# The head of a Mamba-2 trunk kernel: dt and unit 0 interleaved over the tiles of h, the dt and decay turns moved, group 0's exponentials later

## What is computed

```python
h = rms_norm(x, mix_pre_g)
zxbcdt = h @ w_in                       # z 2048, x 2048, B 1024, C 1024, dt 32 columns
xbc = silu(causal_dwconv(xbc, conv_w, conv_b))
dt = softplus(dt_raw + dt_bias)         # (tokens, 32 heads)
a = -dt * exp(a_log)
a_cs = cumsum(a)                        # within a chunk
lmat = exp(a_cs[l] - a_cs[s]), lower triangle
y_diag = (C @ B.T * lmat) @ (x * dt);  states = B.T @ (decay * x * dt);  y_off = C @ prev * exp(a_cs)
```

## Time and profile before

| | |
|---|---|
| median of 3 runs | 1354.79 us (1354.41 to 1354.86) |
| the profiled execution, its own time | 1355.58 us |
| its span, from the first to the last instruction | 1353.8 us |
| TensorE busy | 1333.6 us, 99% |
| VectorE, ScalarE, GpSimd busy | 57%, 42%, 2% |
| the chain that ended last | PE 83%, DVE 7%, ACT 5%, issue 2%, DMA 2% |

### The profile page before, as it was taken

The page is one execution under the profiler, slowest core; times in us unless marked ns, Lnnn a source line. Parts: engine busy times, 40 slices in busy tenths (PEclk is TensorE's granted clock), DMA queues, the critical chain, the costliest instruction groups (busy, mean ns, idle before and its releaser), DMA issues.

```text
span 1353.8 us, 15929 instructions
## 1 busy us (share of the span) xinstructions
PE 1333.6 (99%) x6474; PEld 1115.1 (82%) x6474; DVE 777.9 (57%) x1139; ACT 570.6 (42%) x875; POOL 24.4 (2%) x28
## 2 busy tenths in 40 slices
PE   8999999999999999999999999999999999999998
PEld 6878787877888988888888888888898888888886
DVE  4878778787624666666642266545466656664223
ACT  6666555666324534333331163222453333333112
POOL 0000000000000000000000000000000000000000
PEclk9999999999999999999999999999999999999999
DMA  4532234332242233333343313333223333334331
GB/s 148 162 109 70 89 107 125 110 112 74 79 140 63 63 109 109 94 96 103 97 126 102 115 47 96 104 96 112 91 63 109 108 95 93 94 103 130 93 109 62
DMA packets 181773, 135.70 MB, mean 100 GB/s; under 512 B 5645, under 2 KB 169893, under 8 KB 180677
## 3 DMA queue, kind: packets, MB, share of 16 engines
q1 hardware_dynamic: 181653, 134.62, 33.0%
q10 hardware_dynamic: 48, 0.07, 0.0%
HBM read 132.51 MB, written 2.16 MB: 99 GB/s over the span
## 4 chain that ended last, share of the span: by engine, by line
PE 83%; DVE 7%; ACT 5%; issue 2%; DMA 2%; SPq 0%; DVEq 0%
PE bank L850 17%; PE bank L851 17%; PE bank L852 17%; PE bank L911 9%; PE bank L913 9%; PE bank L912 9%; DMA w_raw<-in_ssd_w_in 2%; DVE mask L637 2%; DVE feat L709 1%; ACT w_hi L355 1%; ACT e_row L428 1%; DVE w_lo L586 1%; PE bank L888 1%; DVE feat L703 1%; ACT L413 1%
## 5 line engine op out<-in xcount | busy, mean ns | idle before, releaser
L850 PE MATMUL bank<-h_hi,w_hi 128*128 128x512 f32 (+1 forms) x1352 | 513.7, 380 | 0.0
L852 PE MATMUL bank<-h_lo,w_hi 128*128 128x512 f32 (+1 forms) x1352 | 511.0, 378 | 0.0
L851 PE MATMUL bank<-h_hi,w_lo 128*128 128x512 f32 (+1 forms) x1352 | 510.8, 378 | 0.0
L586 DVE TENSOR_TENSOR w_lo<-w_raw,w_hi 128x1024 fp32r<-128x1024 f32 x228 | 278.4, 1224 | 356.6 <-ACT w_hi L355 356.5
L355 ACT ACTIVATE w_hi<-w_raw 128x1024 fp32r<-128x1024 f32 x228 | 238.2, 1052 | 203.2 <-PE bank L913 172.8
L852 PEld LDWEIGHTS bank<-h_lo,w_hi 128*128 128x128 f32 x1352 | 254.3, 188 | 47.2
L850 PEld LDWEIGHTS bank<-h_hi,w_hi 128*128 128x128 f32 x1352 | 254.4, 188 | 46.5
L851 PEld LDWEIGHTS bank<-h_hi,w_lo 128*128 128x128 f32 x1352 | 254.4, 188 | 46.3
L911 PE MATMUL bank<-w_hi,hid_hi 128*128 128x512 f32 x416 | 162.4, 390 | 0.0
L913 PE MATMUL bank<-w_hi,hid_lo 128*128 128x512 f32 x416 | 161.9, 389 | 0.0
L912 PE MATMUL bank<-w_lo,hid_hi 128*128 128x512 f32 x416 | 161.8, 389 | 0.0
(11 more groups left out here) (146 smaller groups left out, 944.4 us busy)
## 6 DMA issues: line engine op xcount, KB each, us to landing
w_raw<-in_ffn_w_up SPq DMA_DIRECT2D x88, 512.0 KB, 3.8
w_raw<-in_ssd_w_in SPq DMA_DIRECT2D x48, 512.0 KB, 4.0
w_raw<-in_ffn_w_down SPq DMA_DIRECT2D x44, 512.0 KB, 3.5
w_raw<-in_sc_w_in SPq DMA_DIRECT2D x24, 512.0 KB, 3.7
acs_b<-acs_dram SPq DMA_DIRECT2D x8, 1024.0 KB, 6.2
w_raw<-in_ssd_w_out SPq DMA_DIRECT2D x16, 512.0 KB, 3.5
w_raw<-in_sc_w_out SPq DMA_DIRECT2D x8, 512.0 KB, 3.6
x_tok<-in_x SPq DMA_DIRECT2D x4, 512.0 KB, 4.9
```

What stands on the lines that cost most here:

```text
L586: nc.vector.tensor_tensor(w_lo[slot(u)][:], w_raw[:, u % 2, :], w_hi[slot(u)][:].bitcast(F32), ALU.subtract).then_inc(w_lo_done, 1)
L850: nc.tensor.matmul(dst, wh, xh, start=start, stop=False)
L851: nc.tensor.matmul(dst, wl, xh, start=False, stop=False)
L852: return nc.tensor.matmul(dst, wh, xl, start=False, stop=stop)
```

## The change

- dt: the high and the low weights stand side by side in one tile of 64 columns. Per tile of h two products (with h_hi and with h_lo) give 64 rows; the turn of dt multiplies these rows with a tile `pair` (two unit matrices over each other, made on GpSimd), which adds the halves. The cleared padding and its two memsets go.
- The split of dt's weight comes before the first tile of h on both engines; w_hi 0 and w_lo 0 come behind tile 1.
- TensorE runs the dt products as h_hi and h_lo of a tile come, and unit 0 in the same loop, two tiles behind (LAG). The second set of warm-up products between the transposes goes.
- The turns of dt and of the pages move from unit 0 to unit 1, the cumulative sums from unit 1 to unit 2.
- In group 0, ScalarE does conv_out 2 and conv_in 3 ahead of the exponentials; VectorE does conv 2 ahead of segments(0). The other groups keep their order.

```diff
@@ gpsimd
-            for part in (wdt_hi, wdt_lo):
-                pool.memset(part[:].bitcast(F32)[:, :, HEADS:], 0.0).then_inc(wdt_cleared, 1)
             pool.memset(ones[:], 1.0).then_inc(consts_done, 1)
+            pool.wait_ge(consts_done, 5)
+            pool.tensor_tensor(pair[:], ident[:, 0:HEADS], ident[:, HEADS:2 * HEADS], ALU.add).then_inc(pair_done, 1)
@@ scalar
+            act.wait_ge(wdt_landed, 16)
+            nc.scalar.activation(wdt[:, :, 0:HEADS], wdt_raw[:], ACT.Copy).then_inc(wdt_split, 1)
             act.wait_ge(par1_done, 1)
             for k in range(DT):
                 act.wait_ge(xn_turned, k + 1)
                 nc.scalar.activation(h_hi[:, k, :], bank[k % 6][:], ACT.Copy, scale=one(col_gain(MIX_PRE, 0, k))).then_inc(h0_hi_done, 1)
-                if k == 0:
-                    act.wait_ge(wdt_landed, 16)
-                    act.wait_ge(wdt_cleared, 2)
-                    nc.scalar.activation(wdt_hi[:, :, 0:HEADS], wdt_raw[:], ACT.Copy).then_inc(wdt_split, 1)
-                if k == 3:
+                if k == 1:
                     splits_to(1)
             splits_to(2)
             act.wait_ge(dt_row_mm, 1)
-            nc.scalar.copy(dt_row[:], bank[7][0:HEADS, :]).then_inc(dt_row_done, 1)
+            nc.scalar.copy(dt_row[:], bank[7][0:2 * HEADS, :]).then_inc(dt_row_done, 1)
...
                     conv_in(g, 2, g * XG)
                     conv_out(g, 0)
                     conv_out(g, 1)
+                    conv_in(g, 3, g * XG + 1)
+                    conv_out(g, 2)
                 else:
                     conv_out(g, 0)
                     conv_out(g, 1)
                     conv_in(g, 2, g * XG)
+                    conv_out(g, 2)
+                    conv_in(g, 3, g * XG + 1)
                     exps(g)
                     exps_row(g)
-                conv_in(g, 3, g * XG + 1)
-                conv_out(g, 2)
@@ vector
+            dve.wait_ge(wdt_split, 1)
+            nc.vector.tensor_tensor(wdt[:, :, HEADS:], wdt_raw[:], wdt[:, :, 0:HEADS].bitcast(F32),
+                                    ALU.subtract).then_inc(wdt_split, 1)
...
-                if k == 5:
+                if k == 1:
                     splits_to(1)
...
                 conv(g, 1, CONV_T - GROUPS + g)
+                conv(g, 2, g * XG)
                 if not g:
                     segments(g)
-                conv(g, 2, g * XG)
@@ tensor
-                if c < C - 2:
+                if c == 0:
                     keep_warm(4, 7)
...
             pe.wait_ge(wdt_split, 2)
-            for k in range(DT):
-                pe.wait_ge(h0_lo_done, k + 1)
-                last = three(bank[7][:], wdt_hi[:, k, :], wdt_lo[:, k, :], h_hi[:, k, :], h_lo[:, k, :], k == 0, k == DT - 1)
...
+            hi, lo = w_hi[slot(0)], w_lo[slot(0)]
+            for at in range(DT + LAG):
+                if at < DT:
+                    pe.wait_ge(h0_hi_done, at + 1)
+                    nc.tensor.matmul(bank[7][0:2 * HEADS, :], wdt[:, at, :], h_hi[:, at, :], start=at == 0, stop=False)
+                    pe.wait_ge(h0_lo_done, at + 1)
+                    last = nc.tensor.matmul(bank[7][0:2 * HEADS, :], wdt[:, at, :], h_lo[:, at, :], start=False, stop=at == DT - 1)
...
+                if at >= LAG:
+                    k = at - LAG
+                    if k == 0:
+                        pe.wait_ge(par1_done, 1)
+                        pe.wait_ge(w_lo_done, 1)
+                    cols = slice(k * P, (k + 1) * P)
+                    last = three(bank[GROUP_BANKS[0]][:], hi[:, cols], lo[:, cols], h_hi[:, k, :], h_lo[:, k, :], k == 0, k == DT - 1)
+                    if k == DT - 1:
+                        last.then_inc(unit_done, 1)
...
-                    last = nc.tensor.transpose(bank[4][:, c * HEADS:(c + 1) * HEADS], dt_row[:, c * P:(c + 1) * P], ident[0:HEADS, 0:HEADS])
+                    last = nc.tensor.matmul(bank[4][:, c * HEADS:(c + 1) * HEADS], dt_row[:, c * P:(c + 1) * P], pair[0:2 * HEADS, :],
+                                            start=True, stop=True)
...
-            unit(0, bank[GROUP_BANKS[0]][:], behind={1: turn_dt, 3: turn_pages})
             pe.wait_ge(dt_row_done, 1)
-            unit(1, bank[GROUP_BANKS[1]][:], behind={2: turn_acs})
+            unit(1, bank[GROUP_BANKS[1]][:], behind={1: turn_dt, 3: turn_pages})
...
-                unit(u + 2, bank[GROUP_BANKS[2]][:])
+                unit(u + 2, bank[GROUP_BANKS[2]][:], behind={2: turn_acs} if g == 0 else {})
```

More of the change, by code:

```diff
@@ L147, in build @@
     AHEAD = 3
+    LAG = 2
     acs_dram = nc.dram_tensor("acs_dram", [HEADS, T], F32, kind="Internal").ap()
@@ L205, in build @@
                 wdt_raw = sb("wdt_raw", [P, DT, HEADS], stack=start)
-                wdt_hi, wdt_lo = sb("wdt_hi", [P, DT, P], F32R, start), sb("wdt_lo", [P, DT, P], F32R, start)
-                dt_row = sb("dt_row", [HEADS, T], stack=start)
+                wdt = sb("wdt", [P, DT, 2 * HEADS], F32R, start)
+                pair = sb("pair", [P, HEADS], stack=start)
+                dt_row = sb("dt_row", [2 * HEADS, T], stack=start)
                 a_log_b, dt_bias_b, d_b = (sb(n, [P, HEADS], stack=start) for n in ("a_log_b", "dt_bias_b", "d_b"))
@@ L237, in build @@
             sem(n) for n in ("xn_ready", "xn_turned", "page1_turned", "pages_turned", "par1_done", "par_done"))
-        wdt_cleared, wdt_split, dt_row_mm, dt_row_done = (sem(n) for n in ("wdt_cleared", "wdt_split", "dt_row_mm", "dt_row_done"))
+        pair_done, wdt_split, dt_row_mm, dt_row_done = (sem(n) for n in ("pair_done", "wdt_split", "dt_row_mm", "dt_row_done"))
         dt_mm, dt_act, dt_vec, acs_mm, acs_row_done, acs_tok_done, pads_done = (
@@ L963, in _ @@
-            last.then_inc(dt_row_mm, 1)
+            hi, lo = w_hi[slot(0)], w_lo[slot(0)]
[5 more added lines that the diff above has]
+                    last = nc.tensor.matmul(bank[7][0:2 * HEADS, :], wdt[:, at, :], h_lo[:, at, :], start=False, stop=at == DT - 1)
+                    if at == DT - 1:
+                        last.then_inc(dt_row_mm, 1)
+                    if at + 6 < DT:
+                        for c in range(C):
+                            turned = turn_xn(at + 6, c)
+                        turned.then_inc(xn_turned, 1)
+                if at >= LAG:
[7 more added lines that the diff above has]
+                        last.then_inc(unit_done, 1)
@@ L965, in turn_dt @@
             def turn_dt():
-                pe.wait_ge(dt_row_done, 1)
+                pe.wait_ge(pair_done, 1)
                 for c in range(C):
-                    last = nc.tensor.transpose(bank[4][:, c * HEADS:(c + 1) * HEADS], dt_row[:, c * P:(c + 1) * P], ident[0:HEADS, 0:HEADS])
+                    last = nc.tensor.matmul(bank[4][:, c * HEADS:(c + 1) * HEADS], dt_row[:, c * P:(c + 1) * P], pair[0:2 * HEADS, :],
+                                            start=True, stop=True)
                 last.then_inc(dt_mm, 1)
@@ L983, in turn_acs @@
                 nc.tensor.matmul(bank[3][:, 0:C * HEADS], tri[:], a_tok[:], start=True, stop=True).then_inc(acs_mm, 1)
-            pe.wait_ge(par1_done, 1)
-            unit(0, bank[GROUP_BANKS[0]][:], behind={1: turn_dt, 3: turn_pages})
             pe.wait_ge(dt_row_done, 1)
-            unit(1, bank[GROUP_BANKS[1]][:], behind={2: turn_acs})
+            unit(1, bank[GROUP_BANKS[1]][:], behind={1: turn_dt, 3: turn_pages})
             for g in range(GROUPS):
```

## The result

The changed kernel takes 1367.54 us (median of 5 runs, 1365.84 to 1367.75) against 1354.79: ratio 1.0092, interval 1.0078 to 1.0106, slower by 12.75 us. Forecast were 1362.9 us and a range of 1358.4 to 1366.4. The direction and the path came as predicted; the granted clock of TensorE fell twice where the forecast held it up, and the time lies 1.1 us above the range.

What follows compares the result with a forecast made beforehand. TensorE, busy nearly throughout, bounds the kernel, so the change is worth its shift of group 0's states product: -2.5 (head) + 11.25 (three waits) - 0.6 (short waits absorbed) = +8.1 us, giving 1362.9 us; range 1358.4 to 1366.4.

Steps and rivals of the forecast that it cites:

- What bounds the kernel: TensorE is busy nearly throughout; after group 0 a closed 41.3 us loop repeats, so only the shift of its states product counts.
- The head: Up to unit 1's end: fewer dt products and unit 0 overlapped gain 2.5 us; pages turned at 27.5 against 24.21.
- What is late next: Unit 2 on TensorE waits 3.85 us for w_lo 2; acs_row starts 6.9 us later; unit 3 waits 2.4 us more.
- The exponentials' place: Group 0, second x transposes: SiLU 3 comes late behind the moved exponentials, so TensorE waits 5.0 us.
- The rival that this place doesn't bind: Group 0: SiLU 3 comes earlier than counted, states product at 62.6, +3.6 us, 1358.4 us; chance 0.10.
- The sum: Group 0's states product moves from 59.0 to 67.1, +8.1 us, giving 1362.9 us with all products at full clock.
- the rival of a head that doesn't overlap: Head: unit 0 runs behind dt anyway and ends up to 2.5 us later, 1365.4 us; chance 0.06.
- the one of a gain that reaches the end: Start of unit 2: w_lo 2 is done in time, the head's 2.5 us reach L1021, 1352.3 us; chance 0.05.
- The clock: TensorE behind the two long waits: full clock held; rival of falls at 1.6 us each, 1364.5 or 1366.1, chance 0.25.

Runs made afterwards that it cites:

- all early: Head alone plus dt turn and sums earlier, w_hi 2 and w_lo 2 ahead of the softplus, a_log's Exp ahead of dt_row, page copies behind Ln: 1354.73 us, ratio 0.9998.
- the mask sooner: All early with the sums behind tile 3 instead of 4 of unit 1 and w_lo 4 behind the mask's arguments: 1353.64 us, ratio 0.9989.
- head alone: Changed kernel keeping two dt products per tile and unit 0 in the loop, all turns early again, exponentials in old place: 1356.97 us, ratio 1.0012.
- pages early: Changed kernel with only the parameter pages turned behind tile 3 of unit 0 again: 1365.34 us, ratio 1.0073.
- turns alone: Kernel before with only the turns moved, dt and pages to unit 1, sums to unit 2: 1366.83 us, ratio 1.0088.
- exponentials back: Changed kernel with group 0's exponentials and mask arguments back in their old places on ScalarE and VectorE: 1365.24 us, ratio 1.0070.
- two filled: Changed kernel with warm-up products in TensorE's first and third new wait, 14 ahead of unit 2, 18 ahead of the second x transposes: 1369.44 us, ratio 1.0100.
- early split: Changed kernel with unit 2's weight split (w_hi 2, w_lo 2) ahead of the softplus on both engines: 1362.73 us, ratio 1.0051.
- exponentials' move alone: Kernel before with only group 0's exponentials and mask arguments moved to where the change has them: 1360.06 us, ratio 1.0031.
- three waits filled: Two filled with 8 more warm-up products in the second wait, ahead of unit 3: 1366.49 us, ratio 1.0083.

## Why the prediction was right in its path and wrong in its time

- *What bounds the kernel*: right. The shift of group 0's states product (12.3 us) is the shift of the span (12.1), and it is so in kernels with an undisturbed loop behind it: 0.9 early gives 0.9 (all early), 1.9 gives 2.2 (the mask sooner).
- *The head*: right. The first h_hi started at 11.45 against 11.7, and unit 1's first product at 23.72 against 23.9. The dt turn (0.9 taken) took from 25.17 to 26.18, 1.0 us; the pages turned at 27.67 against 27.5. Unit 1 ended at 30.9 against 30.5, so the head gained 2.1 us, not 2.5.
- *What is late next*: right. The wait for w_lo 2 was 3.65 us against 3.85, the one for w_lo 3 was 2.16 against 2.4. That the split's place behind the softplus is the cause of the first is shown by moving it (the wait gone, 4.8 us less), and that the moved turns are most of the loss by making that move alone (1366.8, of which the waits are 6.9 us).
- *The exponentials' place*: right. TensorE waited 4.5 us there, 5.0 were counted, and the move alone gives the row that was counted (55.56). The rival that this place doesn't bind fell.
- *The sum*: +8.1 us for the order of the queues. With the waits filled it is 8.45. Its terms were off in both directions and partly cancel: the head gained 2.1 us for 2.5, and the three waits of the change come to 10.3 us for 11.25. Unit 1's start took away the rival of a head that doesn't overlap, the wait of unit 2 the one of a gain that reaches the end.
- *The clock*: **this is the step that failed.** "The sum holds all products at full clock", and the falls stood among the rivals with 0.25, at 1.6 us each, so 1366.1 for two. Both happened in the change, and they cost 1.6 and 2.5 us, 3.9 to 4.1 together, where the sum had nothing: the second stretch at 1.2 GHz lasted 6.8 us, twice the 3.4 of the first. My price for a fall came from one stretch at the start of the kernel (3.18 us), as if all were alike, and my chance from waits of 1.2 us, a third or less of the two long new ones (3.65 and 4.53). By the page of the Trainium skill that I weighed (TensorE: Matmul & The Clock Gate, The HAM clock gate), the falls were the expected case, and the trace agrees: 0.50 behind both long waits. I gave its rule a quarter because the trace of before had no wait to show it; the row that spoke for it, the slow first products after an idle start, was there.

The order at 8.45 and the clock at 3.9 make 12.35 us, the shift of the states, by the way they are taken; the check from outside is that the two falls read from the timeline of the change give 4.1. The median is 0.4 us further off, which is within the spread of the runs.

## What to carry to other kernels

When calls are moved behind later work of one engine, follow each of the other engines' programs from the moved call on: here the turns of dt and of the pages (1.0 and 0.45 us) stood ahead of a queue of two table loads, a softplus and a weight split, and the sums ahead of all evictions of group 0. Moving these three by one unit cost 11.6 us by itself, while the saved 1.8 us of products brought no gain in any run until group 0's chain was shortened too. And count a wait of TensorE twice: once as it is, and once for the products behind it, which may run at half the clock; work saved on the engine in front of a fixed wait makes the wait longer, and the head alone cost 1.7 us so.

## What the runs showed of the hardware

- Waits of TensorE of 2.06 and 2.17 us (pages early), 2.16 (turns alone, and exponentials back), 2.19 (two filled) and 2.55 (head alone) were followed by a granted clock of 0.50, while 2.16 us in the change and 2.14 with the early split were not. A wait of 3.12 us at the x transposes was followed by a fall with the pages early and by none in the profiled execution of the exponentials' move alone. Each of the five waits of 3.63 to 4.54 us that were left unfilled had a fall. Among the shorter ones the length alone doesn't decide it; the case doesn't show what does.
- The fall isn't tied to the end of the wait: in these traces it began between 1.5 us before it (early split, third wait) and 1.5 us behind it (two filled, second wait), in the latter case while TensorE was busy.
- Warm-up products in the waits kept the clock at 1.00 through waits that were 3.65, 2.16 and 4.53 us long in the change, without delaying what waited: with three waits filled, 0.36 to 0.54 us of idle was left ahead of each.
- Two falls of the clock in one execution cost 1.6 and 2.5 us. One has no fixed price: the clock was low for 3.4 or for 6.8 us, and a fall cost about half of the time that TensorE worked on the path in it (2.9 and 5.6 us in the change).
- A table load of ScalarE took 1.28 us, and the next activation began 1.29 to 1.30 us behind its start wherever its input was ready (25.47 to 26.77 and 49.99 to 51.29 in the kernel before).
